# The modulation's weight tiles, issued in the step whose output tile computes them

## What is computed

```python
def ada_mod(cv, w, b):
    m = jax.nn.silu(cv) @ w + b
    return jnp.split(m, N_MOD, axis=-1)

# second_block, for both layers, on the latent's and on the context's condition
sh1, sc1, g1, sh2, sc2, g2 = ada_mod(c[:, None, :], ada_w[layer], ada_b[layer])
csh1, csc1, cg1, csh2, csc2, cg2 = ada_mod(c_ctx, ada_w[layer], ada_b[layer])
```

## Time and profile before

| | |
|---|---|
| median of three runs | 3982.86 us |
| the profiled execution, its own time | 3983.27 us |
| its span, first to last instruction | 3981.5 us |
| mean granted TensorE clock | 0.902 |
| TensorE's matmuls busy | 3431.9 us (86%) |
| VectorE busy | 1920.9 us (48%) |
| ScalarE busy | 1166.3 us (29%) |
| SyncE waiting for VectorE's modulation (line 150) | 1009.2 us, 94 times |

### The profile page before, as it was taken

How to read it: one execution, slowest core, us unless ns; L and a number is a source line. 1 busy time by engine, 2 the same in 40 slices (tenths; PEclk the granted TensorE clock), 3 DMA queues, 4 the chain that set the end, 5 groups by cost and what they waited for, 6 DMA issues and landing times. The chain is left out here.

```text
span 3981.5 us, 39909 instructions
## 1 busy us (share of the span) xinstructions
PE 3431.9 (86%) x15798; PEld 2596.8 (65%) x15798; DVE 1920.9 (48%) x3155; ACT 1166.3 (29%) x1928; POOL 17.6 (0%) x14
## 2 busy tenths in 40 slices
PE   7768998897776999897798858799999977999998
PEld 5633576675543377676687533588888864459897
DVE  4564454554564345455644553355345322336464
ACT  3353321121252332122333510132123222333232
POOL 0000000000000000000000000000000000000000
PEclk9877899998886799899899868899999987999999
DMA  4100133332300023333211001212212211012222
GB/s 159 67 0 0 48 127 116 120 118 101 112 11 0 0 96 133 110 127 117 75 63 48 1 15 37 85 59 66 65 61 69 85 33 34 1 58 92 95 95 86
DMA packets 74085, 277.34 MB, mean 70 GB/s; under 512 B 7883, under 2 KB 12491, under 8 KB 72620
## 3 DMA queue, kind: packets, MB, share of 16 engines
q1 hardware_dynamic: 73900, 274.79, 19.9%
HBM read 266.37 MB, written 8.39 MB: 69 GB/s over the span
## 5 line engine op out<-in xcount | busy, mean ns | idle before, releaser
L122 PE MATMUL acc<-normed_hi,weights_hi 128*128 128x512 f32 (+2 forms) x2976 | 1011.6, 354 | 157.2 <-DVE weights_lo L110 118.7
L123 PE MATMUL acc<-normed_lo,weights_hi 128*128 128x512 f32 (+2 forms) x2976 | 1029.1, 351 | 0.0
L125 PE MATMUL acc<-normed_hi,weights_lo 128*128 128x512 f32 (+2 forms) x2976 | 880.6, 350 | 0.0
L104 ACT ACTIVATE weights_hi<-weights_raw 128x1024 fp32r<-128x1024 f32 (+3 forms) x365 | 395.4, 1083 | 1624.7 <-PE acc L125 815.5
L110 DVE TENSOR_TENSOR weights_lo<-weights_raw,weights_hi 128x1024 fp32r<-128x1024 f32 (+3 forms) x365 | 457.9, 1255 | 567.3 <-ACT weights_hi L104 563.9
L122 PEld LDWEIGHTS acc<-normed_hi,weights_hi 128*128 128x128 f32 x2976 | 574.2, 193 | 231.2 <-issue 146.3
L123 PEld LDWEIGHTS acc<-normed_lo,weights_hi 128*128 128x128 f32 x2976 | 573.6, 193 | 73.1
L125 PEld LDWEIGHTS acc<-normed_hi,weights_lo 128*128 128x128 f32 x2976 | 547.6, 192 | 107.4
L122 PE MATMUL acc<-hidden_hi,weights_hi 128*128 128x512 f32 (+1 forms) x880 | 327.7, 381 | 50.7 <-DVE weights_lo L110 43.2
L123 PE MATMUL acc<-hidden_lo,weights_hi 128*128 128x512 f32 (+1 forms) x880 | 333.4, 379 | 0.0
L125 PE MATMUL acc<-hidden_hi,weights_lo 128*128 128x512 f32 (+1 forms) x880 | 302.1, 375 | 0.0
(11 more groups left out here) (301 smaller groups left out, 3779.1 us busy)
## 6 DMA issues: line engine op xcount, KB each, us to landing
weights_raw<-in_w_up SPq DMA_DIRECT2D x176, 512.0 KB, 4.0
ada_tiles<-in_ada SPq DMA_DIRECT2D x96, 512.0 KB, 3.5
weights_raw<-in_w_down SPq DMA_DIRECT2D x64, 704.0 KB, 4.4
weights_raw<-in_w_in SPq DMA_DIRECT2D x67, 512.0 KB, 4.1
weights_raw<-in_w_out SPq DMA_DIRECT2D x32, 512.0 KB, 3.3
x_kept<-x SPq DMA_DIRECT2D x2, 3072.0 KB, 9.7
x<-x_kept SPq DMA_DIRECT2D x1, 3072.0 KB, 11.0
weights_raw<-in_mla_down SPq DMA_DIRECT2D x6, 512.0 KB, 3.4
```

Of the source, the lines that this page charges most:

```text
L104: act.activation(self.hi[:, n % 2, 0:w], self.raw[:, n % 2, 0:w], ACT.Copy).then_inc(self.high_ready, 1)
L122: pe.matmul(out, self.hi[:, s, m], xh, start=k == 0, stop=False)
L123: pe.matmul(out, self.hi[:, s, m], xl, start=False, stop=False)
L125: mm = pe.matmul(out, self.lo[:, s, m], xh, start=False, stop=k == kt - 1)
```

## The change

The two calls in `Start` go. Nothing else is edited; but since `load` counts its own calls, each later call issues the tile with a number smaller by two, with the wait that belongs to that number: step j now loads the tile that step j computes, and waits for the compute of two tiles before.

```diff
@@ -2311,8 +2311,6 @@
         Z.R.load(sp, 1)
         sp.dma_start(K["consts"], ins["consts"]).then_inc(Z.kept, 16)
         sp.dma_start(M.cond[:], ins["conditions"].partition_broadcast(P)).then_inc(Z.x_back, 16)
-        M.load(sp)
-        M.load(sp)
         sp.dma_start(X[:, :, 0:CTX], ins["ctx"]).then_inc(Z.stored, 16)
         sp.dma_start(K["rope"], ins["rope"]).then_inc(Z.stored, 16)
```

## The result

The changed kernel takes 3723.96 us (median of four runs, 3719.82 to 3731.71), the kernel before 3982.3 us beside it: 258 us less, a ratio of 0.936 with a 95% interval of 0.935 to 0.938. The prediction was 3727 us, in a range of 3705 to 3780. The profiled execution of the changed kernel took 3719.82 us, with a span of 3718.0.

A forecast was written before the change was run, and what follows sets the result against it. The prediction took a closed loop of SyncE, weight transfer, ScalarE and VectorE as the bound; stretch gains of 255.9 us off a 3981.5 us span gave 3725.6, plus 1.8 around it: 3727 us, range 3705 to 3780.

The forecast's parts named there:

- The bound: In stages with modulation, a closed loop through SyncE, weight transfer, ScalarE and VectorE: 11.03 us per Residual step against TensorE's 7.43.
- The two calls removed: In Start, two 512 KB transfers no longer stand ahead of ctx and rope: counted 0, bounds 0 to 2.4 us gain.
- The wait in its place: VectorE's possible wait for modulation tiles: 8.8 us of room in InProjection, landing in 3.1 to 4.2, costed at nothing.
- The pace: In stages with modulation, TensorE sets the step without the loop: 5.60 us per 1024-input tile, 7.43 per 1408-input tile.
- The sum: Gains added by stretch over both projections and both networks, less 0.7 us at the end: 255.9 us.
- seven stretches: Two projections, two network beginnings, two networks and the way into the second projection: 33.4, 35.0, 5.9, 6.0, 81.7, 77.6, 17.0 us gain.
- the passage: From the first network's last step to the second projection's fourth tile: 44.5 us before, 27.5 after, gain 17.0.
- The check from the other side: TensorE's 146.5 us of weight waits, 12 hidden, plus low-clock loss: near 250 us, the clock a third of the gain.
- 3837 and 3797 us: In the modulation stages, waits vanish but the clock returns nothing (3837) or under 40 us (3797); together 7 in 100.
- Late tiles: Modulation tiles land late in the projections and Residual: about 3810 us at 14.1 us landing, 4210 at 25; 2 in 100.
- That nothing happens: SyncE's modulation wait has another reason, the loop running through split, so time stays at 3983 us; 2 in 100.
- The upper bound: Over the whole kernel, 0.3 us of waiting in each of 126 steps and three low-clock passages: 47 us more, 3774.

The follow-up runs named there:

- the added matmuls: Kernel before the change, with 10 further matmuls ahead of the weights' wait in 45 projection and Residual steps with modulation: 3987.09 us, ratio 1.001.

## Why the prediction was right

- **The bound.** Read rightly: a closed loop SyncE, DMA, ScalarE, VectorE. Three experiments part it from its rivals: the modulation in another queue (all of the gain), one step less of lead (all of the gain), the same wait with the weights ahead (a third).
- **The two calls removed.** Counted at 0; the fourth tile is emptied at 42.11 against 41.85 us, 0.3 us later. The gain of up to 2.4 us that I kept as a bound wasn't there.
- **The wait in its place.** Counted at nothing, with 4.6 us to spare. Right: VectorE has no wait for `ada_tiles` in the changed kernel, whose 96 tiles landed so:

```profile
DMA to landing us min/median/max: 3.0/4.3/6.7
```

  I had taken the landings from the kernel before, 3.1 to 4.2 us. In the projections they stayed near that (3.1 to 4.5, with 8.8 us of room); in the networks they rose to a median of 4.3 and at most 6.7 us. The experiment that holds each tile until the one before was computed shows that the cover is larger than I worked out, because VectorE's lag is itself covered.
- **The pace.** The tiles of 1024 inputs come 5.60 us apart, as counted. Most steps with 1408 inputs take 7.48 us, not the 7.43 of the one pair of rows that I took; but the first two of each `Residual` take 7.28 and 7.41, so the eight are 0.13 us over the sum. The last pair of each `Up` takes 11.51 us instead of 11.2. The two together, twice in a network, are the 0.9 us by which each network took longer.
- **The sum.** The seven stretches gave 252.5 us against 256.6. The term that was mis-sized is the passage: I took it from a passage without modulation and added the wait of VectorE alone. The wait became a stop of TensorE of 2.4 us, and that brought the low clock, 2.9 us more: 30.0 us against 27.5.
- **The check from the other side.** Its reading was wrong, that the clock is a third of the gain. Stops and low clock added up to nearly the right sum because together they fill the loop's turn, and not because each has its price: where the added matmuls took the clock from 0.86 and 0.92 to 0.99 and 1.00, the steps stayed as long. The sum wasn't made from it, so the time came out right.
- **The rivals.** For 3837 and 3797 us I had priced stops and clock apart. The Trainium skill ("TensorE: Matmul & The Clock Gate", section "What's actually happening") puts the ramp under 1% of a typical span. Where the clock is on the path, what was measured is of that size: 11 to 27 us of 3725 in the two attentions and 2.9 in the passage. What the low clock costs in the rest of the program, whose mean in the changed kernel is 0.921, no run shows. What misled was adding a price of the clock to that of the stops. Late tiles: no landing over 6.7 us, and none waited for. That nothing happens: excluded by the result.
- **Span against forecast.** 3718.0 measured, 3725.6 forecast. The stretches gave 4.1 us less than the sum, the mixers 14.9 us that were the clock's alternation, and the rest of the program took 2.9 us more than I had allowed, where it lies between 2086 and 2096 us in all profiles; what moves it there was not tried. The median, 3724, is nearer to the forecast than the steps behind it deserve, and that is luck: a profile with mixers at 331 us would have had a span of about 3733.
- **Slips that changed nothing.** The upper bound counts 126 steps; there are 142 (110 with 1024 inputs, 32 with 1408), which makes 3779 instead of 3774, still inside the range. The 0.37 us between the two transfers stand in the earlier trace rows, not in rows 4.

## What to carry to other kernels

When one queue issues two streams, ask of each wait in it what stands behind it and whether that is ready: a prefetch issued two steps early may be blocked until a buffer of the present step is free, and then holds back a transfer that has all it needs. Issue a transfer where its condition is already met, or in a queue of its own; a longer lead isn't a safer one. And take the price of a loop from its turn: in it, an engine that has time to spare may be slow at no cost, while the same slowness on the path of the work costs in full. An average over stages hides this; read the clock and the steps where the loop is closed.

## What was unexpected of the hardware

- A stop of 2.4 us of TensorE cost 2.9 us more, as the matmuls after it started 0.43 instead of 0.23 us apart for the next 7 us.
- In an attention with some fifteen stops of TensorE of up to 1.2 us, the granted clock alternates between its two levels, with a mean of 0.70 to 0.78 in executions of the same code (0.78 and 0.74 for the changed kernel), and this is 7 us of 117. Two matmuls of 128 columns ahead of each of 32 waits held it at 0.99 from 305 us on and made the whole program 29 us faster.
- Stops of TensorE of 0.5 to 0.8 us in `Up` (at 561.95, 574.13 and 586.06 us in the kernel before) left the clock at 1.00.
- A weight tile of 704 KB issued 0.37 us behind one of 512 KB took 4.7 us to ScalarE's start, alone ahead of it 4.1.
